# Order of scores and values in the unit loops of three attentions, in a two-block model on one core

## The reference

```python
def attend(q, k, v, bias=None, mask=None, sink=None):
    s = jnp.einsum('...qngd,...knd->...ngqk', q, k).astype(jnp.float32) * (HEAD_DIM ** -0.5)
    ...
    p = jax.nn.softmax(s, axis=-1)
    ...
    return jnp.einsum('...ngqk,...knd->...qngd', p.astype(v.dtype), v)
```

## Time and profile before

| | us |
|---|---|
| median of three runs | 3806.12 |
| lowest, highest | 3800.87, 3807.11 |
| profiled execution, its own time | 3797.35 |
| its span, first to last instruction | 3795.5 |
| MLA, first layer and second | about 201 to 340 and 1241 to 1380 of the span |
| NA | about 2329 to 2473 |
| SWA | about 3226 to 3377 |

### The profile page before, as it was taken

One profiled execution on the slowest core, in us unless ns is written; L12 is line 12 of the kernel. 1 busy time (PEld: TensorE's weight loads), 2 busy tenths in 40 slices (PEclk: granted clock), 3 DMA queues, 4 the chain that ended last, 5 costly groups with the idle time before them and its releaser, 6 DMA issues.

```text
span 3795.5 us, 58344 instructions
## 1 busy us (share of the span) xinstructions
PE 3663.5 (97%) x19742; PEld 2985.5 (79%) x19742; DVE 2165.3 (57%) x3292; ACT 1860.3 (49%) x3571; POOL 1772.5 (47%) x1395
## 2 busy tenths in 40 slices
PE   8999899999999988999999999999999999999999
PEld 7866688788888666887888887778888987678887
DVE  4567642788535676427885764742235957743234
ACT  4555544444445555444344545744444653754443
POOL 4423573556544235735565453065563235025564
PEclk9999999999999999999999999999999999999999
DMA  4210241455222102414553322132223542012222
GB/s 143 89 62 29 73 139 62 155 190 187 94 89 89 62 29 73 145 62 153 195 183 106 128 95 95 46 106 96 97 95 104 174 161 78 2 43 91 94 95 88
DMA packets 106907, 388.48 MB, mean 102 GB/s; under 512 B 11856, under 2 KB 11984, under 8 KB 106320
## 3 DMA queue, kind: packets, MB, share of 16 engines
q1 hardware_dynamic: 87840, 318.81, 24.5%
q10 hardware_dynamic: 16416, 57.62, 4.4%
q0 software_dynamic: 2448, 9.36, 0.7%
HBM read 383.64 MB, written 2.10 MB: 102 GB/s over the span
## 4 chain that ended last, share of the span: by engine, by line
PE 69%; issue 15%; DVE 7%; POOL 6%; ACT 2%; DMA 0%; POOLq 0%; ACTq 0%; DVEq 0%; SPq 0%
PE ps L676 18%; PE ps L678 18%; PE ps L677 18%; POOL arena_parts L640 3%; PE ps L1163 2%; POOL arena_parts L644 1%; PE ps L1182 1%; PE ps L1171 1%; DVE rstd L2135 1%; PE ps L2200 1%; POOL lines L431 1%; PE ps L1141 1%; PE ps L2210 1%; PE ps L907 1%; PE ps L848 1%
## 5 line engine op out<-in xcount | busy, mean ns | idle before, releaser
L677 PE MATMUL ps<-arena_parts 128*128 128x512 f32 (+1 forms) x3156 | 1174.3, 372 | 0.0
L640 POOL TENSOR_TENSOR arena_parts<-ring,arena_parts 128x512 fp32r<-128x512 f32 x492 | 655.5, 1332 | 1021.4 <-ACT arena_parts L617 817.8
L676 PE MATMUL ps<-h_parts,arena_parts 128*128 128x512 f32 x2096 | 822.8, 393 | 10.1 <-POOL arena_parts L640 7.2
L678 PE MATMUL ps<-h_parts,arena_parts 128*128 128x512 f32 x2096 | 816.6, 390 | 0.0
L644 POOL TENSOR_TENSOR arena_parts<-ring,arena_parts 128x512 fp32r<-128x512 f32 x492 | 664.7, 1351 | 282.2 <-ACT arena_parts L626 281.6
L677 PEld LDWEIGHTS ps<-arena_parts 128*128 128x128 f32 x3156 | 596.1, 189 | 104.3 <-issue 2.4
L1663 DVE SCALAR_TENSOR_TENSOR conv<-ps,cols,conv 128x511 f32<-128x511 f32 (+3 forms) x536 | 377.6, 705 | 525.0 <-ACT conv L1678 371.3
L617 ACT ACTIVATE arena_parts<-ring 128x512 fp32r<-128x512 f32 x574 | 361.2, 630 | 640.5 <-PE ps L678 595.0
L626 ACT ACTIVATE arena_parts<-ring 128x512 fp32r<-128x512 f32 x574 | 360.2, 628 | 589.4 <-PE ps L678 553.2
L676 PEld LDWEIGHTS ps<-h_parts,arena_parts 128*128 128x128 f32 x2096 | 394.3, 188 | 97.0 <-POOL arena_parts L640 8.1
L678 PEld LDWEIGHTS ps<-h_parts,arena_parts 128*128 128x128 f32 x2096 | 394.2, 188 | 82.4
(11 more groups left out here) (357 smaller groups left out, 6450.4 us busy)
## 6 DMA issues: line engine op xcount, KB each, us to landing
ring<-in_stream SPq DMA_DIRECT2D x606, 512.0 KB, 3.2
ctx<-in_mod ACTq DMA_DIRECT2D x48, 512.0 KB, 3.3
sq<-in_mod ACTq DMA_DIRECT2D x48, 512.0 KB, 3.3
sq<-in_bias POOLq DMA_DIRECT2D x8, 512.0 KB, 4.5
conv<-in_bias POOLq DMA_DIRECT2D x8, 512.0 KB, 4.5
arena<-in_mem ACTq DMA_DIRECT2D x2, 1024.0 KB, 4.7
out_y<-x ACTq DMA_DIRECT2D x8, 256.0 KB, 2.7
x<-in_x SPq DMA_DIRECT2D x4, 256.0 KB, 4.7
```

What stands on the lines that cost most here:

```text
L640: eng.tensor_tensor(side_of(lin, i, c, 0, to), side_of(lin, i, c, 0, raw), side_of(lin, i, c, 0, top), ALU.subtract)\
L676: pe.matmul(out, w_h, x_h, start=start, stop=False)
L677: pe.matmul(out, w_h, x_r, start=False, stop=False)
L678: return pe.matmul(out, w_r, x_h, start=False, stop=stop)
```

## The change

In both loops the scores of the coming unit are issued ahead of the values of the past one. Before, an iteration issues values, scores, transposes; after, scores, values, transposes. The waits of each step move with it, and nothing else is changed: all other engines' lists, the buffers and the number of instructions are the same. The second hunk is `duo_pe`, which NA and SWA share. MLA runs the first hunk in each of two layers.

```diff
--- before.py
+++ after.py
@@ -1190,10 +1190,10 @@
                 fill = {0: q0, 1: q1, 3: k, 4: v} if p + 1 < PAIRS else {}
                 for n in range(MLA_UNITS):
                     u = p * MLA_UNITS + n
+                    if u + 3 < len(units):
+                        scores(units[u + 3])
                     if n % 2 and u >= 3:
                         values(units[u - 3], units[u - 2])
-                    if u + 3 < len(units):
-                        scores(units[u + 3])
                     turn(units[u])
                     if n in fill:
                         fill[n]()
@@ -2239,10 +2239,10 @@
                 wait(pe, name, value)
             scores(1)
             for n in range(N):
+                if n + 2 < N:
+                    scores(n + 2)
                 if n >= 2:
                     values(n - 2)
-                if n + 2 < N:
-                    scores(n + 2)
                 turn(n)
             values(N - 2)
             values(N - 1)
```

## The result

The changed kernel takes 3816.74 us (median of 8 runs, 3811.23 to 3819.25), the kernel before 3802.84 beside it (8 runs, 3798.32 to 3807.11): a ratio of 1.0035 with a 95% interval of 1.0025 to 1.0045, 13.9 us slower. The forecast was +14.0 us; its 3820.1 stands on a median of the kernel before that has moved to 3802.84 with more runs.

The account below looks back on a forecast made before the run. PE, busy 97% of the span, was taken as the bound, so time moves where it waits. Form changes 0, MLA -1.4, NA +5.5 and SWA +9.9 gave +14.0 us: 3820.1 on the 3806.12 median, range 3804 to 3829.

Parts of the forecast that it names:

- Form changes: PE in all stages: each change of matmul form costs about 0.1 us, their number stays; 0, between -13 and +13 us.
- rival of dearer forms: Scores ahead of values costs another 0.1 us at 130 places on top of the forecast: 3833 us; chance 0.08.
- MLA, -1.4: Last head pair of each MLA layer: the swap closes PE's wait on L1244, -0.7 us per layer, bounds 0 and -2.8.
- NA, +5.5: One new wait of scores per pair where two context units precede a latent one: 6 times 0.85, once about 0.45.
- SWA, +9.9: Two new waits per pair and one old one gone: 7 x 1.77 less 6 x 0.41 us.
- (a): SWA, first new wait per pair: scores of unit 24 wait 0.70 us for late exponentials of unit 22.
- (b): SWA, second new wait per pair: scores of unit 26 wait 1.07 us for late exponentials of unit 24.
- (c): SWA: the present wait at 3297.07, 0.41 us against the usual hand-over, goes because scores of unit 25 come later anyway.
- first rival: NA and SWA: DVE's output and maximum not serial on the path, only MLA's 1.4 us left: 3804.7; chance 0.12.
- rival of a gain: NA and SWA: DVE takes the next maximum while values run, SWA's six 0.41 waits go; -3.9 us, 3802.2; chance 0.05.
- a granted clock that falls within SWA: Sign against the forecast: clock, 1.00 now, falling in SWA where new waits thin PE's work; no size given.

Follow-up runs that it names:

- e5: Changed kernel, with DVE's L1971 work for the context output in NA moved to the fourth unit of the next pair; one execution, 3815.86 us.
- e7: Changed kernel, with each DVE output in NA and SWA one iteration later, behind the next maximum, and extra buffer places; 3800.05 against 3801.63 us before, 0.9997.
- e10: Changed kernel with two places for values and spread sums, output waiting for values first, DVE's order as in the change; 3826.01 against 3801.13 us before, 1.0066.
- e8: Changed kernel, with DVE's output waiting for all values before it copies the inverse row; 3833.27 against 3801.13 us before, 1.0084.
- e1: Kernel before with only the first hunk of the change (MLA); 3798.24 against 3801.63 us, 0.9994.
- e2: Kernel before with only the second hunk of the change (NA and SWA); 3821.24 us, 1.0051, 19.6 us more.
- e11: Kernel before, with DVE's output waiting for all values before it copies the inverse row; 3809.23 against 3801.13 us, 1.0020.
- e12: Repeat of e11 in a further session; 3809.25 against 3801.98 us before, 1.0021.
- e6: Changed kernel, with values in front again in the iterations of NA and SWA where PE waits; 3800.05 against 3801.63 us before, 1.0000.
- e9: Kernel before (values ahead of scores) with e7's late outputs and extra places; 3803.49 against 3801.13 us, 1.0005.

## Why the prediction was right

**Form changes, 0: right.** In NA and SWA, V starts 0.07 to 0.08 us ahead of the modelled end of the scores (2397.51+1.14 against 2398.57), like the changes of form before, and so it is at all of the new places in NA, SWA and MLA. In MLA, transposes followed by scores, the same form, still start 0.16 to 0.17 ahead. Scores ahead of values has no price of its own, and the rival of dearer forms (3833) falls. What the Trainium skill, page "TensorEngine Tiling (Array Packing)", Tiling Modes, Key Properties, says of a drain at a change of tiling mode fits: every change of form costs the same 0.1 us here, whichever two forms it is between, and their number has not changed.

**MLA, -1.4: right in kind, undersized.** The wait on L1244 went as worked out. But each stage is 0.97 us shorter and not 0.70, -1.9 in all. The wait at 330.97 was 0.70 as shown, but 0.76 against the usual early start, a correction that the forecast made in SWA and left out here. The rest is a second, smaller gap, which has no bracket in PE's row. V at 327.36 starts 0.14 us behind the modelled end of the transpose ahead of it, where 0.06 ahead is usual. It waited for ACT's copy (L1296), which ends at 327.31. The copy and the transpose, before:

```profile
326.71 0.60 ACT L1296 ACTIVATE quarters<-ps 128x512 f32<-128x512 f32 x1 [0.37 <-PE ps L1171]
...
326.95 0.27 PE L1171 MATMUL ps<-const,conv 128*128 128x128 f32 x1
```

After, V at 327.33 stands behind scores (326.59+0.81) and starts 0.07 ahead of their end: PE works through the time of that wait. 0.76+0.20 is 0.96 of the 0.97. So the swap closes two waits per layer, where the forecast said one.

**NA, +5.5: measured +5.6.** The wait is where it was put, once per pair behind two context units. It is 0.80 (0.73 shown), not 0.85: from the start of L1971 to the bias add are 0.32 us, since the two overlap in the records, and the forecast took the operation's whole 0.40. In pair 0, which has no L1971 there, it is 0.47 (0.39 shown; forecast 0.45). e5, which moves L1971 away, shows a wait shorter by 0.34. The forecast had not named the last of the 5.6, a wait of 0.26 (0.18 shown) in the last pair.

**SWA, +9.9: measured +9.6.** The two waits are 0.71 and 1.07 (0.64 and 0.99 shown) against 0.70 and 1.07; the 0.33 of before is gone. A pair takes 1.37 more, and (a), (b) and (c) made 1.36. The 0.3 too much is the first wait (a), which is only 0.30 (0.23 shown) in the pair behind the half-clock stretch.

**The cause.** In the forecast, V's new place makes DVE's out late, and the top behind it in the list late with it. e7 takes this one link away and the whole loss goes; e10 keeps the buffers and the loss stays; e8 lengthens the link and the loss grows by 0.51 us per pair in both stages. Against the first rival, nothing measurable, the forecast said that DVE starts each top right behind an out. That holds in the earlier trace rows for the one at 3296.24 alone; those at 2398.78 and 3291.09 waited for the scores (0.31 and 0.63 in brackets). What holds against it is the order of the list, and after the change the rows: the bias adds at 2400.60 and 3312.61 come without a wait behind a late out and what DVE does after it. The rival of a gain (3802.2) named its own condition, that out stands behind the top. e7 makes that condition true, and yet the old wait of 0.41 in SWA does not go (17.88, as before), so this half of the rival was wrong even so. e7's time alone can't say how much gain is left: it is 1.6 us below the kernel before, but its runs have a lower granted clock, and at the same clock they are 4.5 to 5.2 below. Its stages account for 2.7 of that, 1.9 in MLA and 0.8 in NA; the rest is open.

**The sum.** That 14.0 met 13.9 so closely is partly luck: the median moves by a few microseconds from session to session, and half-clock time, which the forecast left out but for a line in its last part, moved by 24 us between the two profiled executions. At the same granted clock the difference is 10.2 to 12.6 us, against 13.3 by the stages. The forecast named a granted clock that falls within SWA as a sign against it: the clock did fall, but at the stage's start and not where the new waits are, and e1, with the old order there, has such a start too.

## What to carry to other kernels

When a step is moved on one engine, read the lists of the others for what stands in order behind its result. Here V came later by the length of one scores group, nobody was waiting for the output, and yet the next unit's maximum stood behind it in DVE's list, and the exponentials and scores behind that. Moving the consumer back too, with a buffer more, took the loss away (e7), but brought the pairs of NA and SWA nothing over the kernel before: NA's scores had no wait to lose, and SWA's only moved by one unit. And compare a periodic stage by its period at full clock, where 0.02 us can be told, not by the kernel's time alone, where a few microseconds go with the clock.

## What was not expected of the hardware

Much of what the runs of one kernel differ by goes with the granted clock. Each run has a mean granted clock, known to three digits. Mean times in us of the runs at each clock, with their number (before: 63 runs from the three sessions of the experiments):

| clock | before | after | e1 | e2 | e7 | e11, e12 |
|---|---|---|---|---|---|---|
| 0.986 | 3798.6 (9) | | 3795.4 (2) | | | |
| 0.985 | 3801.1 (31) | 3811.3 (2) | | | | |
| 0.984 | 3803.0 (18) | 3815.6 (3) | 3799.1 (7) | 3818.6 (2) | 3797.8 (3) | |
| 0.983 | 3805.9 (3) | 3818.0 (2) | 3802.1 (2) | 3821.2 (1) | 3801.4 (7) | 3808.8 (8) |

In the kernel before, 0.001 of the clock goes with 2 to 3 us, in every session. So medians of two kernels whose runs differ in clock differ by that too, and a row of this table is the fairer comparison, good to a microsecond or two. It can't say which is cause: a kernel with new waits may be granted less because of them.

The clock of a stage is not fixed by the stage's own instructions either. The granted clock over the first 20 us of SWA was 1.00 in the profiled executions of before, e6 and e10, 0.74 in e1, e9, e11 and e12, and 0.66 in after, e2, e5, e7 and e8. e1's SWA has the instructions of before in the order of before, and it takes 155.5 us where that takes 151.0. Its first 20 us:

```profile
3222.70:3242.70 20.00, 17.89 (x100) 12.14 (x99) 10.64 (x29) 11.10 (x25) 0.00 (x0) 0.74 0.00 1
```

PE is as busy in them as in the kernel before at full clock (17.89 us of the first 20 there too, 3226 to 3246), but gets through fewer instructions:

```profile
3226.00:3246.00 20.00, 17.89 (x134) 12.37 (x134) 14.25 (x40) 14.92 (x34) 0.00 (x0) 1.00 0.00 1
```

Which event starts such a stretch can't be read from these traces.

The steady part of SWA stays at 1.00 in the changed kernel, waits and all. In e8 and e10, with 0.51 more per pair, half-clock stretches appear within the steady part. In e8 some pairs take 20.1 to 21.4 us instead of 19.76, and the mean clock of 3255 to 3372 is 0.97; in e10 it is 0.99.

```profile
3255.00:3372.00 117.00, 104.46 (x896) 75.44 (x896) 73.72 (x224) 74.63 (x179) 0.00 (x0) 0.97 0.00 1
```

So part of e8's 32.1 us is the clock and not the waits themselves. The third case stays open: e11 and e12, with no steady pair longer, are 7 to 8 us slower in both sessions, with some 32 and 35 us more at half clock than the profiled execution of before.
